# Ten weight buffers moved by 64 bytes in SBUF, in a two-block transformer forward pass

## The reference

```python
# first block
h = rmsnorm(x, g); proj = h @ w_in            # then two kinds of attention with softmax
x = x + rmsnorm(concat(o_nsa, o_swa) @ w_o, g)
gu = rmsnorm(x, g) @ w_gate_up                # 1024 -> 5632
...
x = x + rmsnorm((gelu(conv(a)) * u) @ w_down, g)
x = x + (p @ w_ple) * sigmoid(x @ w_ple_gate)
# second block
proj = rmsnorm(x, g) @ w_in_2                 # neighbourhood attention and retention
x = x + concat(na, ret) @ w_out_2
x = x + square(relu(rmsnorm(x, g) @ w_up_2)) @ w_down_2    # 1024 -> 4096 -> 1024
return rmsnorm(x, g)
```

## Time and profile before

| | us |
|---|---|
| median of 3 runs | 1295.25 (1295.04 to 1295.27) |
| span of the profiled execution, first to last instruction | 1293.9 |
| PE busy | 1278.1 |
| PE weight loads busy (beside the matmuls) | 1063.6 |
| DVE, ACT, POOL busy | 802.8, 635.7, 155.7 |

### The profile page before, as it was taken

The page is one execution under the profiler, slowest core; times in us unless marked ns, Lnnn a source line. Parts: engine busy times, 40 slices in busy tenths (PEclk is TensorE's granted clock), DMA queues, the critical chain, the costliest instruction groups (busy, mean ns, idle before and its releaser), DMA issues.

```text
span 1293.9 us, 16698 instructions
## 1 busy us (share of the span) xinstructions
PE 1278.1 (99%) x6136; PEld 1063.6 (82%) x6136; DVE 802.8 (62%) x1559; ACT 635.7 (49%) x1243; POOL 155.7 (12%) x146
## 2 busy tenths in 40 slices
PE   9999999999999999999999999999999999999998
PEld 8888888878888888888778777889888888888887
DVE  6699799685655565346788886578644343344334
ACT  6787576454335343234555655476543252342344
POOL 0022120000110011001002101022311030110111
PEclk9999999999999999999999999999999999999999
DMA  8211110433332333322323212432333323232321
GB/s 276 82 50 42 33 42 17 164 87 91 91 104 76 112 98 98 97 92 77 110 90 105 74 58 59 127 107 83 93 94 98 92 81 114 82 111 86 105 90 66
DMA packets 64624, 118.20 MB, mean 91 GB/s; under 512 B 7712, under 2 KB 12192, under 8 KB 64288
## 3 DMA queue, kind: packets, MB, share of 16 engines
q1 hardware_dynamic: 62704, 112.86, 28.7%
q10 hardware_dynamic: 1840, 4.29, 1.1%
HBM read 115.02 MB, written 2.10 MB: 91 GB/s over the span
## 4 chain that ended last, share of the span: by engine, by line
PE 87%; DVE 7%; issue 2%; ACT 2%; DMA 1%; POOL 0%; SPq 0%; POOLq 0%; DVEq 0%; ACTq 0%
PE bank L581 26%; PE bank L583 26%; PE bank L582 25%; PE bank L801 2%; PE bank L681 1%; PE bank L683 1%; PE bank L682 1%; DVE pp L2156 1%; PE bank L787 1%; PE bank L788 1%; DVE wl L1985 1%; DVE ptl L2178 1%; DVE pp L2173 1%; DMA raw<-in_w_swa 1%; DVE qs L2072 1%
## 5 line engine op out<-in xcount | busy, mean ns | idle before, releaser
L1985 DVE TENSOR_TENSOR wl<-raw,wh 128x512 fp32r<-128x512 f32 (+2 forms) x360 | 266.0, 750 | 326.6 <-ACT wh L1291 326.0
L1291 ACT ACTIVATE wh<-raw 128x512 fp32r<-128x512 f32 (+1 forms) x398 | 242.3, 619 | 287.6 <-PE bank L583 274.7
L581 PE MATMUL bank<-AH,wh 128*128 128x512 f32 (+1 forms) x848 | 333.0, 393 | 2.7 <-DVE AL L1999 0.8
L583 PE MATMUL bank<-AH,wl 128*128 128x512 f32 (+1 forms) x848 | 328.9, 388 | 0.0
L582 PE MATMUL bank<-AL,wh 128*128 128x512 f32 (+1 forms) x848 | 326.7, 385 | 0.0
L581 PE MATMUL bank<-BH,wh 128*128 128x512 f32 x624 | 248.4, 398 | 0.0
L583 PE MATMUL bank<-BH,wl 128*128 128x512 f32 x624 | 245.1, 393 | 0.0
L582 PE MATMUL bank<-BL,wh 128*128 128x512 f32 x624 | 243.8, 391 | 0.0
L581 PEld LDWEIGHTS bank<-AH,wh 128*128 128x128 f32 x848 | 159.5, 188 | 36.5 <-issue 4.0
L583 PEld LDWEIGHTS bank<-AH,wl 128*128 128x128 f32 x848 | 159.2, 188 | 35.3
L582 PEld LDWEIGHTS bank<-AL,wh 128*128 128x128 f32 x848 | 159.4, 188 | 33.0 <-issue 0.2
(11 more groups left out here) (336 smaller groups left out, 1632.0 us busy)
## 6 DMA issues: line engine op xcount, KB each, us to landing
raw<-in_w_dn SPq DMA_DIRECT2D x104, 256.0 KB, 2.6
raw<-in_w_gu SPq DMA_DIRECT2D x88, 256.0 KB, 2.6
raw<-in_w_up SPq DMA_DIRECT2D x64, 256.0 KB, 2.6
raw<-in_w_nsa SPq DMA_DIRECT2D x16, 256.0 KB, 2.6
raw<-in_w_pg SPq DMA_DIRECT2D x16, 256.0 KB, 2.7
raw<-in_w_naq SPq DMA_DIRECT2D x16, 256.0 KB, 2.6
nbi<-in_na_bias ACTq DMA_DIRECT2D x8, 448.0 KB, 3.3
raw<-in_w_swa SPq DMA_DIRECT2D x10, 256.0 KB, 3.0
```

The costliest lines, as they stand in the source:

```text
L581: t.matmul(o, w, xh, start=start, stop=False, skip_group_check=skip)
L583: return t.matmul(o, wl, xh, start=False, stop=stop, skip_group_check=skip)
L1291: a.activation(W[i % NW].h[:, 0:n], RAW[i % NRAW][:, 0:n], ACT.Copy).then_inc(*s_wh.up(i))
L1985: v.tensor_tensor(w.l[:, 0:n], RAW[i % NRAW][:, 0:n], w.h[:, 0:n], ALU.subtract).then_inc(*s_wl.up(i))
```

## The change

The counter is moved on by 64 bytes before the ten weight halves, and by 64 bytes again before `AH`, while `cst` gives up 256 bytes (it needs less than 192 columns):

```diff
         RAW = [new(f"raw{i}", 512) for i in range(NRAW)]
+        top[0] += 64
         W = [Pair(new(f"wh{i}", 512, F32R), new(f"wl{i}", 512, F32R)) for i in range(NW)]
...
-        cst = new("cst", 256)
+        cst = new("cst", 192)
...
         a_tmp = [new(f"tmp{i}", T + 2) for i in range(5)]
+        top[0] += 64
         aA = region(8192)
...
-            assert c_used[0] <= 256
+            assert c_used[0] <= 192
```

## The result

| | us |
|---|---|
| before, median of 4 runs | 1295.26 (1295.04 to 1295.59) |
| after, median of 4 runs | 1308.78 (1307.90 to 1310.40) |
| ratio | 1.0109, 95% interval [1.0097, 1.0121] |
| span of after's profiled execution; its own time | 1306.1; 1307.9 |

The change costs 13.5 us, where 10 us less was forecast; the median lies above the forecast range. The own time of after's profiled execution is 1.8 us above its span.

The account below looks back on a forecast made before the run. It took PE's matmul count times their distance as the bound; gains of 10.0, 1.3 and 0.6 us minus 0.7 and 1.2 us back made 10.0 us less, 1285.2 us, with a range of 1282 to 1300.

Parts of the forecast that it names:

- What bounds the kernel: Whole kernel: PE is busy 99% of the span at nearly full clock, so time is matmul count times their distance.
- The three paces: 512-column matmuls in the trace before: 229.0 ns usually, 233.3 in six stretches and swapped lines, 226.7 with both operands at 64.
- the 35 x 6 at 230.0: Stream starts: some 35 entries, six matmuls each at 230.0 ns instead of 226.7 while settling; 0.7 us back.
- all at 64: Lines 581 to 583: both operands at 64 modulo 128 give 226.7 ns instead of 229.0; 10.0 us less.
- The small tiles at nothing: `ident`, `ones`, `tmp`, `r_bc`, `cst` and `dn` change place, used by DVE, ACT, POOL and short fp32 matmuls; costed at nothing.
- The swapped lines: Lines 681 to 683, activations stationary and weights moving: 192 matmuls go from 233.3 to 226.7 ns; 1.3 us less.
- The give-back of 1.2 us: Where DVE sets the pace, faster matmuls only wait longer; 1.2 us back, including attention tiles already at 64.
- No effect: Rival for the whole kernel: the change leaves the time as it was, durations 392 ns on average; chance 0.12.
- Never settling: Rival for every stream of triples: distances stay at 230.0 ns, 4.4 us more minus 0.6, 1299 us; chance 0.16.
- The long pace: Rival: all streams take 233.3 ns, 18.8 us more, 1314 us; chance 0.14.

Follow-up runs that it names:

- the equal kernel: Kernel before with `cst` cut to 192 columns and 192 bytes before `AH`, so weights and activations both begin at 128 modulo 256; 1285.08 us.
- The kernel with `wl` alone apart: Kernel before with `cst` cut and halves allocated apart: `wh`, `AH`, `AL` at 128 modulo 256, `wl` at 0; 1302.05 us.
- D = +96: Kernel before with `cst` cut and 96 bytes before `AH`: weights (moving) at 128, activations (stationary) at 32 modulo 256; 1314.71 us.

## Why the prediction was wrong

**What bounds the kernel** was read rightly. The time is a number of matmuls times their distance; the span of after differs mostly by what the two long streams differ.

**The three paces** were real, and 226.7 ns is indeed a pace into which whole streams settle: 1285.08 us in the equal kernel against the 1285.2 forecast. Settling takes up to ten matmuls, much as the 35 x 6 at 230.0 assumed.

**The step that failed** is the condition for that pace: it was read off matmuls with their tiles "all at 64" modulo 128, and so weights at 64 modulo 128 would give it to all. Both at 64 modulo 128 is the 226.7 pair (192 and 192) and also the pair that the change makes (192 and 64). The two kernels with both operands at 192, and with 192 and 64, are 24 us apart (1285.8 and 1310.1). What decides is D modulo 256. The trace had the means to see it: `pth` moving at 64 against `vl` at 192 has D = 128, with 395 ns, and all three lines of after last 395 ns. The prediction named that row and then set it aside, since the matmuls follow a start closely. Taken as a duration, by 395 - 162.4 = 232.6 ns, it would have given 4,350 x 3.6 = 15.7 us more, 1311, against 1308.8 measured. But that agreement is partly luck. `ptl` against `vh` has the same D of 128 in before, and there the duration is that of a faster matmul:

```profile
L582 PE MATMUL bank<-ptl,vh 128*128 128x512 f32 x16 | 6.3, 391 | 0.0
```

The mean of the two, 393 ns, gives 230.6 ns and 1302 us. The rows with the relation of after said slower, and not by how much. The ruler itself holds for a mean over all lines of a stream and not for one line: the 397 ns of the earlier trace rows would give 234.6 ns where the starts give 233.3.

**A step that the paces share.** The two paces that were named beside the usual one, 226.7 and 233.3 ns, lie 6.67 ns apart, and they are 34 and 35 times that. A settled stream repeats a pattern, and in each of these kernels the sum over the pattern is a whole multiple of 6.67 ns. By the starts from 300 to 630 us before has 1,440 distances in 329.60 us; they repeat every three (about 231, 226 and 229 ns), which makes 686.7 ns, 103 x 6.67. The kernel with `wl` alone apart has 1,427 in 329.80 us, repeats every three too, and comes to 693.3 ns, 104 x 6.67. After's second stream has 1,290 in 299.78 us from 950 to 1250 us, repeating every seven: 1,626.7 ns, 244 x 6.67. At D = +96 it is 1,408 in 329.88 us, every seven: 1,640.0 ns, 246 x 6.67. So each pace between 226.7 and 233.3 ns, and the one above, is a whole number of such steps over three or seven matmuls. What a step is isn't shown; a D of 32 bytes costs the same 233.3 ns as one of 64.

**The small terms.** The small tiles at nothing: right (1.0000 [0.9990, 1.0009]). The swapped lines were forecast to fall from 401 ns to about 390. They stand at 401 in after, and at 395 in the equal kernel, in the groups with shapes apart:

```profile
L683 PE MATMUL bank<-wh,BH 128*128 128x512 f32 x64 | 25.7, 401 | 0.0
```

```profile
L682 PE MATMUL bank<-wh,BH 128*128 128x512 f32 x64 | 25.3, 395 | 0.0
```

The give-back of 1.2 us where DVE sets the pace can't be told from the other small terms. The part between the long streams takes 300.2 to 300.6 us at D = -64 with the clock undisturbed, 302.3 in after and 297.9 in the equal kernel, which gains 2.3 to 2.8 us there. Part of that is its streams which stood at 233.3 ns in before and run at 226.7 there.

**The rivals.** No effect, at 1295.3, is refuted by twelve kernels, after among them, that stand 0.5% or more above or below it. That addresses do something is shown: with the same instructions and the clock at 1.00 in both long streams (weight loads busy for 1063.6 and 1063.8 us before and after), D alone moves the distance of 512 columns from 226.7 to 234.3 ns. Whether it is the weight load that takes the time isn't shown. Never settling had the right cue, modulo 256, and too small a price (230.0). The long pace, 1314, was nearest in size: after's two patterns are 232.4 and 233.3 ns. So the slower side happened, which the prediction gave 0.30; its cue for it, the pair modulo 256, was the right one, though it took it for streams that never settle, and these settle on a slow pattern.

**What stays open.** Only the relative place of the two operands counts, the sign included (228.9 ns at D = -64, 233.3 at +64), and the swapped roles follow the same rule (229.0 ns at -64, 233.3 at +64). What makes the pace depend on it isn't shown: no run took the weight load away from beside the matmul. Nor is it shown why D = 128 has two patterns, why a few short streams at D = -64 run at 233.3 ns, or why with `wl` alone apart two products of three are long.

## What to carry to other kernels

Where a kernel is a long stream of float32r matmuls with a weight load for each, give the stationary and the moving tiles the same place modulo 256 bytes (here 226.7 ns a matmul, against 228.9 to 234.3 at the seven other D that were tried); check it in the built addresses, with padding before one group, for both roles and for every tile of the stream (one operand of three apart already cost 17 us here). If a rule on addresses is read from a few matmuls of a trace, tabulate every pair by its difference modulo the largest period at hand before the condition is named, and price all the rows that have exactly the relation the change will make. Before two executions are compared part by part, compare the granted clock of each part: 3.5 us at half clock hid a loss of 1.6 to 2.1 us here. Being aligned alone means nothing: 128 and 0 were slow (1306.90 us), 160 and 160 fast (1285.82).

## What the runs showed that I had not expected

- The distance of 512-column float32r matmuls depends on D modulo 256 with a sign: 228.9 ns at -64 and 233.3 at +64. 32 bytes off equal already costs the full 2.0% over equal places (1310.71 and 1311.47 against 1285.08).
- At D = 128 one kernel runs its streams at 232.4 or 233.3 ns. A long stream of 1,488 matmuls differs by 1.4 us between them; which it takes varies between kernels with the same D: the first long stream runs at 233.3 ns in after (1,416 matmuls in 330 us) and at 232.3 in the kernel with 128 and 0 (1,422).
- Single executions differ by the clock, whatever their D. The profiled one of the kernel with the weights alone moved begins slowly. Its first twelve matmuls of 408 columns, in groups of four, and the thirteenth:

```profile
5.55 1.70 PE L670 MATMUL bank<-wh,AH 128*128 128x408 f32 x4 [0.75 <-ACT wh L1293]
...
9.58 0.35 PE L683 MATMUL bank<-wh,AH 128*128 128x408 f32 x1
```

  They take 4.03 us, and in after 2.32:

```profile
5.96 0.98 PE L670 MATMUL bank<-wh,AH 128*128 128x408 f32 x4 [1.15 <-ACT wh L1293]
...
8.28 0.45 PE L683 MATMUL bank<-wh,AH 128*128 128x408 f32 x1
```

  Behind the first distance nine are 340 ns; in after they are about 185 ns. That is 1.84 times as long, and in the stretch of before at a granted clock of 0.51 the distances are 0.43 us, 1.86 times the 229 ns of a granted 1.00; so I take this start for one at half clock, which is an estimate. The granted clock reads 1.00 from 5.5 to 8.5 us there, but this is no reading of the clock: the trace's first record of it begins at 9.34 us, at the full level, and there the distances fall to about 185 ns. In all sixteen traces the distances are short from the start where that record begins before 5.4 us, and 340 ns where it begins at 9.0 us or later. The same execution has a second slow stretch, with matmuls of 512 columns 0.43 us apart:

```profile
780.50:784.50 4.00, 4.00 (x12) 0.57 0.00 0
```

  The slow start leaves it 1.3 us behind after (9.58 against 8.28), and the second stretch costs some 1.4 us more (seven distances of 0.43 instead of 0.23 us); together that is about the 2.5 us by which its span (1308.6) is above after's (1306.1). Four of the sixteen profiled executions have such a stretch, between 772 and 785 us: before and the kernels with D at 128 (the weights alone), +64 and -32. The two long streams, on which the paces rest, stand at a granted clock of 1.00 in all of them.
